# Six projection slots of the second mixer layer computed with seven block products instead of eight

## What is computed

```python
for l in range(DEPTH):
    need_ctx = l < DEPTH - 1
    ...
    h = rmsnorm(x, norm1_g[l]) * (1.0 + sc1) + sh1
    hc = rmsnorm(xc, norm1_g[l]) * (1.0 + sc1c) + sh1c
    y, yc = token_mixers(h @ w_in[l], hc @ w_in[l], ...)
    x = x + g1 * (y @ w_out[l])
    h = rmsnorm(x, norm2_g[l]) * (1.0 + sc2) + sh2
    x = x + g2 * sq_relu_mlp(h, w_mlp1[l], w_mlp2[l])
...
qm, km, vm, om, qn, kn, vn, gm = jnp.split(p, cuts, axis=-1)   # 7 parts of 512 columns, and the gates
```

## Time and profile before

| | |
|---|---|
| median of 3 runs | 3272.93 us (3271.8 to 3273.28) |
| the profiled execution: its time, its span | 3277.99 us, 3276.2 us |
| PE busy, mean granted clock of PE | 3241.6 us (99% of the span), 0.998 |
| DVE, POOL, ACT busy | 2052.1, 1069.0, 738.5 us |

### The profile page before, as it was taken

The page is one execution under the profiler, slowest core; times in us unless marked ns, Lnnn a source line. Parts: engine busy times, 40 slices in busy tenths (PEclk is TensorE's granted clock), DMA queues, the critical chain, the costliest instruction groups (busy, mean ns, idle before and its releaser), DMA issues. The chain is left out here.

```text
span 3276.2 us, 40858 instructions
## 1 busy us (share of the span) xinstructions
PE 3241.6 (99%) x15664; PEld 2491.7 (76%) x15664; DVE 2052.1 (63%) x3725; ACT 738.5 (23%) x1589; POOL 1069.0 (33%) x834
## 2 busy tenths in 40 slices
PE   8999999999999999999999999999999999999999
PEld 5767775555555567778888878888886887888888
DVE  8766677676765623278555678566535688866543
ACT  3432422010101333141111134211111235321111
POOL 0111323323232010215666500344441552344443
PEclk9999999999999999999999999999999999999999
DMA  7334412333331121232455334322222221122222
GB/s 270 133 100 129 126 52 78 115 122 110 116 104 63 61 89 49 88 97 83 151 178 180 116 122 155 109 89 80 90 90 103 82 87 45 40 78 90 91 90 90
DMA packets 71650, 339.14 MB, mean 104 GB/s; under 512 B 9024, under 2 KB 21696, under 8 KB 41248
## 3 DMA queue, kind: packets, MB, share of 16 engines
q1 hardware_dynamic: 59120, 303.28, 26.9%
q0 software_dynamic: 6528, 18.75, 1.8%
q10 hardware_dynamic: 5808, 14.49, 1.4%
HBM read 315.91 MB, written 14.42 MB: 101 GB/s over the span
## 5 line engine op out<-in xcount | busy, mean ns | idle before, releaser
L3072 POOL TENSOR_TENSOR scratch<-ring 128x512 f32<-128x512 f32 (+1 forms) x156 | 220.0, 1410 | 1391.6 <-PE psum L791 1048.1
L791 PE MATMUL psum<-big,scratch 128*128 128x256 f32 (+1 forms) x2240 | 606.9, 426 | 0.0
L791 PEld LDWEIGHTS psum<-big,scratch 128*128 128x128 f32 x2240 | 425.6, 190 | 163.7
L791 PE MATMUL psum<-H,scratch 128*128 128x256 f32 (+1 forms) x2312 | 536.9, 387 | 0.0
L791 PEld LDWEIGHTS psum<-H,scratch 128*128 128x128 f32 x2312 | 438.4, 190 | 83.9 <-issue 7.9
L791 PE MATMUL psum<-big,ring 128*128 128x256 f32 (+1 forms) x1584 | 421.5, 418 | 4.4 <-DVE cb L2307 3.0
L791 PE MATMUL psum<-H,ring 128*128 128x256 f32 (+1 forms) x1648 | 422.5, 399 | 1.7 <-issue 0.7
L791 PEld LDWEIGHTS psum<-big,ring 128*128 128x128 f32 x1584 | 300.2, 190 | 108.9 <-DVE cb L2307 4.6
L791 PEld LDWEIGHTS psum<-H,ring 128*128 128x128 f32 x1648 | 311.3, 190 | 80.5 <-ACT H L1663 6.4
L1556 ACT ACTIVATE cb<-psum 128x256 f32<-128x256 f32 x357 | 136.8, 384 | 1029.2 <-PE psum L791 1019.4
L3073 POOL TENSOR_TENSOR scratch<-ring 128x512 f32<-128x512 f32 (+1 forms) x156 | 219.5, 1407 | 0.0
(11 more groups left out here) (407 smaller groups left out, 4240.7 us busy)
## 6 DMA issues: line engine op xcount, KB each, us to landing
ring<-in_wall SPq DMA_DIRECT2D x202, 1024.0 KB, 4.9
big<-in_wada SPq DMA_DIRECT2D x48, 512.0 KB, 3.4
big<-in_wada POOLq DMA_DIRECT2D x32, 512.0 KB, 4.1
big<-in_wall SPq DMA_DIRECT2D x11, 1024.0 KB, 6.9
early_sums<-big SPq DMA_DIRECT2D x11, 1024.0 KB, 8.7
scratch<-early_sums SPq DMA_DIRECT2D x11, 1024.0 KB, 4.8
big<-in_wada SPq DMA_DIRECT2D x8, 1024.0 KB, 20.9
scratch<-in_rpb ACTq DMA_DIRECT2D x16, 512.0 KB, 4.1
```

Of the source, the lines that this page charges most:

```text
L791: mm = pe.matmul(fast_bank(st, q, b), lhsT, rhs(k), start=start and k == 0, stop=k == kt - 1, skip_group_check=True)
L3072: pool.tensor_tensor(s1, a21, a22, ALU.add).then_inc(combo_own, 1)
```

## The change

Slots 1, 2, 4, 6, 7, 10 of layer 1 (`PROJECTED`) are computed with 7 products of 4 matmuls, over 384 tokens (keys) or 256 (queries), in the banks 0, 1, 2 (`fast_project`), and are not paired with the following slot. ACT copies products 1, 5, 6 straight to the output tiles, and the last product; DVE adds products 2, 3, 7 to them in place. The input differences are made once (`project_mixes`, 16 DVE operations) in the place of X: SP sends the 512 columns of X to device memory (`residual`, 2 MB) before, and brings them back when slot 10 is done. The weight sums go to `cb`, one buffer (`project_weights` on POOL, waiting for product 7 of the slot before). ACT's column-ordered copy `order_by_columns` moves from behind slot 0 into slots 1 and 2. The numbering of later stages shifts by 6. The core of the diff:

```diff
+PROJECTED = (1, 2, 4, 6, 7, 10)
+PX = Stage("proj", True, 50, 36, 2, 0, 0, -1, 1, 8)
...
+        project_sums = cb[:, 0:SLOT].rearrange("p (i k c) -> p i k c", i=4, k=4)
+        def query(s):
+            return s in (0, 2, 10, 11)
+        def project_width(s):
+            return 256 if query(s) else 384
+        def project_half(s, k, a):
+            return H6[:, k, 2 + a::2, :] if query(s) else H6[:, k, a::2, :]
+        def project_mix(s, i, j):
+            at = (4 * i + j) * 384
+            return X_[:, at + 384 - project_width(s):at + 384]
...
+                if n == 52:
+                    sp.wait_ge(c21_done, PX.q0)
+                    sp.dma_start(residual, X[:, :, CTX:TOK]).then_inc(residual_out, 16)
+                if n == 50 + PROJECTED[-1] + 3:
+                    sp.dma_start(X[:, :, CTX:TOK], residual).then_inc(residual_back, 16)
...
+            def fast_project(s, middle, after):
+                x = PROJECTED.index(s)
+                q, n, r = PX.q0 + x, project_width(s), wait_slot()
+                assert (w.slot, w.fast) == (PX.slot0 + s, q)
...
+                pe.wait_ge(acc_free[0], w.unit // 2)
+                product(2, 0, block(1, 0), raw(1, 0), True)
+                pe.wait_ge(acc_free[1], w.unit // 2)
+                product(1, 1, block(0, 0), raw(0, 0), True)
+                middle(0)
+                pe.wait_ge(combos_ready, sums_made_by_pool(q))
+                product(5, 2, total(0), mixed(0), True)
+                pe.wait_ge(copied[1], q + 1)
+                product(6, 1, total(1), mixed(1), False)
+                after(0)
+                pe.wait_ge(copied[5], q + 1)
+                product(3, 2, total(3), raw(1, 1), False)
+                pe.wait_ge(copied[6], q + 1)
+                product(7, 1, total(2), mixed(2), False)
+                middle(1)
+                pe.wait_ge(c22_done, q + 1)
+                product(4, 1, block(1, 1), mixed(3), False)
+                after(1)
...
+            def fast_project(l, s):
...
+                copy(1, 0, 0, 1).then_inc(copied[1], 1)
+                mixer_point(l, 4 * s)
+                copy(5, 1, 1, 2).then_inc(copied[5], 1)
+                copy(6, 0, 1, 1).then_inc(copied[6], 1)
+                if s in (1, 2):
+                    order_by_columns(l, range(4 * s - 4, 4 * s))
+                mixer_point(l, 4 * s + 1)
+                mixer_point(l, 4 * s + 2)
+                w.unit += 2
+                if s > 5:
+                    swap_halves(l, s, 0)
+                act.wait_ge(c22_done, q + 1)
+                copy(4, 1, 0, 1).then_inc(acc_free[1], 1)
+                act.wait_ge(acc_free[1], w.unit // 2)
+                act.sem_inc(c21_done, 1)
+                if s > 5:
+                    swap_halves(l, s, 1)
+                mixer_point(l, 4 * s + 3)
...
+            def project_mixes():
+                dve.wait_ge(residual_out, 16)
+                for i in range(4):
+                    for j in range(4):
+                        if i < 2:
+                            dve.wait_ge(h_ready, 16 + 4 * i + j + 1)
+                        if i in (1, 3):
+                            dve.wait_ge(mixed_ready, 16 * PX.mix + 4 * (i // 2) + j + 1)
+                        def half(h, a):
+                            return H6[:, 4 * h + j, a::2, :]
+                        def mix(m):
+                            return project_mix(1, m, j).rearrange("p (t c) -> p t c", c=P)
+                        x, y = ((half(0, 1), half(0, 0)), (half(1, 1), mix(0)), (half(1, 1), half(0, 1)), (half(1, 0), mix(1)))[i]
+                        dve.tensor_tensor(mix(i), x, y, ALU.subtract).then_inc(mixed_ready, 1)
+            def add_product(s, i, also, f, a, b):
+                q, scale = PX.q0 + PROJECTED.index(s), HD ** -0.5 if query(s) else 1.0
+                dve.wait_ge(prod[i], q + 1)
+                dve.wait_ge(copied[also], q + 1)
+                for to, product in projected(s, f, a, bank(b)):
+                    if query(s):
+                        ins = dve.scalar_tensor_tensor(to, product, scale, to, ALU.mult, ALU.add)
+                    else:
+                        ins = dve.tensor_tensor(to, product, to, ALU.add)
+                return ins
+            def project_first(s):
+                add_product(s, 2, 1, 0, 0, 0).then_inc(c11_done, 1)
+            def project_others(s):
+                q = PX.q0 + PROJECTED.index(s)
+                add_product(s, 3, 6, 0, 1, 2).then_inc(c12_done, 1)
+                dve.wait_ge(c12_done, q + 1)
+                dve.wait_ge(c11_done, q + 1)
+                dve.sem_inc(acc_free[0], 1)
+                add_product(s, 7, 5, 1, 1, 1).then_inc(c22_done, 1)
...
+            def gates(l, midway=lambda: None):
...
+                midway()
...
+                    project_mixes()
+                def first_project():
+                    if l and 1 in PROJECTED:
+                        project_first(1)
+                        project_others(1)
+                gates(l, first_project)
                 if l:
+                    if 2 in PROJECTED:
+                        project_first(2)
+                        project_others(2)
                     decay_size()
...
+                    fast = l and pt // 4 > 2 and pt // 4 in PROJECTED
+                    if fast and pt % 4 == 0:
+                        project_first(pt // 4)
+                    if fast and pt % 4 == 2:
+                        project_others(pt // 4)
...
+            def project_weights(s):
...
+                pool.wait_ge(prod[7], PX.q0 + x)
+                pool.tensor_tensor(s1, a21, a22, ALU.add).then_inc(combo_own, 1)
+                pool.tensor_tensor(s3, a11, a21, ALU.subtract)
+                pool.wait_ge(combo_own, mixes + 1)
+                pool.tensor_tensor(s2, s1, a11, ALU.subtract).then_inc(combo_own, 1)
+                pool.wait_ge(combo_own, mixes + 2)
+                pool.tensor_tensor(s4, a12, s2, ALU.subtract).then_inc(combos_ready, 1)
...
+                    for slots, masks in (((1,), (0,)), ((2, 4), (1, 2, 3, 4, 5)), ((6,), (6, 7)), ((7, 10), ())):
+                        for slot in slots:
+                            if slot in PROJECTED:
+                                project_weights(slot)
+                        for h in masks:
+                            add_mask(h)
```

More of the change, by code:

```diff
@@ L130 @@
 FAST = {st.slot0 + x: st.q0 + x for st in STAGES for x in range(len(st.slots()))}
+FAST.update({PX.slot0 + slot: PX.q0 + x for x, slot in enumerate(PROJECTED)})
 class Walk:
@@ L876, in fast_stage, with product, block, total @@
                 w.fast += len(slots)
+            def fast_project(s, middle, after):
+                x = PROJECTED.index(s)
+                q, n, r = PX.q0 + x, project_width(s), wait_slot()
+                assert (w.slot, w.fast) == (PX.slot0 + s, q)
+                def product(i, b, weights, rhs, start):
+                    for k in range(4):
+                        mm = pe.matmul(bank(b, n), weights(k), rhs(k), start=start and k == 0, stop=k == 3, skip_group_check=True)
+                    mm.then_inc(prod[i], 1)
+                def block(h, f):
+                    return lambda k: slot_cols(r, 4 * h + k, f * P, P)
+                def total(i):
+                    return lambda k: project_sums[:, i, k, :]
+                def raw(h, a):
+                    return lambda k: project_half(s, 4 * h + k, a)
+                def mixed(i):
+                    def of(k):
+                        if x == 0:
+                            pe.wait_ge(mixed_ready, 16 * PX.mix + 4 * i + k + 1)
+                        return project_mix(s, i, k)
+                    return of
+                pe.wait_ge(acc_free[0], w.unit // 2)
[16 more added lines that the diff above has]
+                after(1)
+                w.slot += 1
+                w.unit += 2
+                w.fast += 1
             def project_tokens(lhs, with_ctx, after=None, middle=None):
@@ L1373, in after @@
                         mixer_point(l, 4 * s + 2 * f + 1)
-                    if s in VALUE_SLOTS:
+                    if l and s in PROJECTED:
+                        fast_project(s, middle, after)
+                    elif s in VALUE_SLOTS:
                         pe.wait_ge(hc_ready, DT * (l + 1))
@@ L1605, in fast_stage, with copy @@
                 w.fast += len(slots)
+            def fast_project(l, s):
+                x = PROJECTED.index(s)
+                q, scale = PX.q0 + x, HD ** -0.5 if query(s) else 1.0
+                def copy(i, f, a, b):
+                    act.wait_ge(prod[i], q + 1)
+                    for to, product in projected(s, f, a, bank(b)):
+                        ins = act.activation(to, product, ACT.Copy, scale=scale)
+                    return ins
[7 more added lines that the diff above has]
+                mixer_point(l, 4 * s + 2)
+                w.unit += 2
+                if s > 5:
[4 more added lines that the diff above has]
```

(27 more changed lines are left out.)

52 lines of the change are left out of this document (36 added, 16 removed).

## The result

The changed kernel takes 3279.48 us (median of 20, 3275.25 to 3285.64), the kernel before 3272.92 in the same series; the ratio is 1.0019 (95% interval 1.0012 to 1.0026). That is 6.6 us slower by the medians, at the edge of the 0.2% that the prediction takes for the least that can be told, against +2.5 forecast.

The account below looks back on a forecast made before the run. PE, busy 99% of the span, was taken as the bound. -13.66 + 2.5 + 1.2 + 6.7 + 0.5 + 1.9 + 3.4 = +2.5 us gave 3275.5 us; own range 3270 to 3281, with the other cases 3265 to 3284.

Parts of the forecast that it names:

- The gain: Fewer matmuls gain 2.58 us in each of four wide slots, 1.67 in each of two query slots: 13.66 together.
- The head: Head of layer 1: POOL's sums slow DVE's updates and squares; norm, H and slot 0 come 2.5 us later.
- My slower rival: Each new wait (slot 1, slot 2, pt 44) brings the clock down: 10.2 instead of 3.4, 3282.2 us, chance 0.24.
- Slot 1: Ahead of product 4, PE waits 1.2 us until DVE has added product 7.
- the input differences: Sixteen DVE operations take 7.6 us ahead of the gates, where DVE idles 8.92: cost 0.
- X's way to memory: Moving X out takes 7.3 us, and X is final some 10 us before H: no cost.
- that rival: X's transfer back takes 1.0 us longer than 7.3 and moves the recurrence: some 4 us, 3279.5, chance 0.04.
- Slot 2: PE waits for DVE's scans, gates and additions: 2.1 undisturbed, 1.8 and 2.8 through POOL's sums, in all 6.7 us.
- The 8.7 us worked out with the lock: Slot 2's wait if each of POOL's four sums holds up a scan by about 0.94: 2.1 + 3.8 + 2.8.
- The upper bound of 8.3: Slot 2's wait if POOL's sums slow the scans 2.7 times, too: 8.3 us.
- Slot 10: Its gain of 1.67 is lost at pt 44, where PE waits for `rope`: +1.9 us, of 1.0 to 4.0.
- The clock: One fall of the granted clock, 3.4 us; bounds 0 and 10.2 (slots 1, 2 and pt 44).

Follow-up runs that it names:

- the late sums: Changed kernel with POOL's sums of slot 1 waiting until the norm has written two tiles of H: 3273.96 us, ratio 1.0003.
- e7_moves_reload: `e6_three_moves` with SP's load of X put behind the recurrence's query weights, not ahead of them: 3265.96 us, ratio 0.9981.
- e3_scans_first: Changed kernel with DVE making the first three scans ahead of slot 1's additions of products 3 and 7: 3272.04 us, ratio 0.9996.
- e6_three_moves: Changed kernel with slot 1's POOL sums later, three scans first, and slot 4's sums after slot 2's additions: 3265.34 us, ratio 0.9977.

## Why the prediction was right, and where it was off

**The gain** was right: slots 4, 6 and 7 give 6.49 net of 0.7 that the clock still takes in slot 3, so 7.2 of 7.74 (0.5 for the waits there had been taken).

**The head** was the step mis-sized. "2.5 us later" was the wait, 2.60 measured, and the squares took what the earlier trace rows said. Left out was that the clock falls behind this wait: 5.94 instead of 2.5, 3.3 us more, given back by the late sums. I looked for falls at slots 1, 2 and pt 44 only, though the first profile of before has one at the head. My slower rival had the right mechanism and the wrong place: the first and the last of these three waits (0.97, 1.57) did not bring the clock down in either profile.

**Slot 1** was right (0.97 for 1.2), and the input differences and X's way to memory cost nothing: the sixteen differences end at 1132.4, 1.7 us ahead of the gates. X's way back took 12.3 us, not 7.3, which is past the limit of that rival (1.0 longer), but the 4 us that the rival put on it did not come: with the transfer behind the query weights the time is no shorter (`e7_moves_reload`).

**Slot 2** was right in place and nearly in size: 0.63 + 5.91 waiting for 6.7, and 2.5 of clock for 3.4 (4 us at 0.50, 4 at 0.87). That the wait came out so near is partly luck, as the working inside was off twice, against each other. The scans and the step behind lost 3.1 to POOL, not 1.8, since each step loses about 0.9 whatever its length, and the end of the gates lost 2.1, not 2.8. The Trainium skill's "SBUF — State Buffer", section "Who interferes with whom", has the port pair locked for a whole instruction. The flat price agrees with that and not with my rate per column, and POOL's second sum beside the scans is held as well (2.71 instead of 1.3). The 8.7 us worked out with the lock did not come either: the four steps lost 3.1 and not 3.8, the end of the gates 2.1 and not 2.8, and PE itself came 0.63 later. The upper bound of 8.3 does not follow from its own rates: scans slowed 2.7 times lose 2.8 in 4.4 us, and 2.1 + 2.8 + 2.8 is 7.7.

**Slot 10** was right, and in its mechanism: it nets 0.00 for +0.23, as `rope` of tile 4 ends no earlier though PE is ready earlier. With seven products the first half of the tile is ready later, since it needs products 1, 2, 3 and 6: ACT sends its swapped copy 11.9 us after the slot began, not 7.8. But this is not what `rope` goes by. It starts 16.4 to 17.8 us after the slot began with seven products and 16.6 to 17.4 with 16 matmuls, and ends at the same two distances, beside POOL's steps. That POOL slows it there was in the earlier trace rows (1.18 and 1.46 instead of 0.69), and the prediction did not read it.

**The clock** was forecast with one fall, 3.4; there were two, in both profiles. That was one of the prediction's own signs of being wrong, and it had a price for it, +5.9. With 3.3 us for the second one the sum is +5.8, against +6.6 by the medians. So 3279.48 lies in the forecast's own range because that reaches 5.5 us above its middle, not because the account with one fall held. No length of wait tells where the clock falls: behind one of 1.39 it stood at 0.61 and 0.53 for 8 us (`e3_scans_first`, at 1431.38), behind 2.62 at pt 44 at 1.00 (`e6_three_moves`). The rest, and the spread of the changed kernel (10 of 20 executions lie above 3280), is not explained stage by stage; falls that come and go behind the later waits, as in the earlier trace rows, are the candidate and were only argued.

**Two readings** of before were off and change no term. ACT is busy 23% of the span, not about a third. And DVE's gates do have a break: in that trace DVE waits 2.33 us for ACT before 1130.75.

## What to carry to other kernels

Removing matmuls from a bound engine pays only where what they hid has cover of its own: here three slots inside the attention paid their 7.2 us, and three at its edges (the two query slots and the one behind the norm) gave nothing or took more. Price every new wait of PE together with the clock behind it, as a term of its own and at every place. And ask whether the step that PE meets next moves with PE: at pt 44 it did not, and the gain became a wait. Then look for idle time on the engine that is late: three scans moved into a gap of 3.8 us, and sums moved off a busy DVE, made of +0.19% a -0.23%.

## What was not expected of the hardware

A collision of POOL's sums of 512 columns with DVE steps on two operands in SBUF costs DVE 0.8 to 1.07 us a step, for a step of 6 columns and scans of 256 as for scans of 768. With a longer step of POOL the price is higher, and either side can pay it. Mask 0 (1024 columns, 1.96 us alone) met the input differences: with the sums late, one difference that started just behind it took 2.32 instead of 0.55 (at 1122.42), and in the changed kernel the mask itself took 5.99, to 1134.25, past the last difference (1132.4), while these lost nothing. Two profiles of one unchanged kernel differ by 7.4 us in span (3276.2 and 3268.8): by a wait of 1.59 and one of 0.94 that only one has, and by the falls of the clock.
